# A decoder layer with 32 experts: the rings of raw expert weights hold two slots instead of three

## What is computed

```python
def _trunk_layer(x, mod, conv_buf, s0, lb, ...):
    u = x * (1.0 + scale1) + shift1
    p = u @ w_in                                   # short convolution | gated recurrence
    ...
    x = _layer_norm(DEEPNORM_ALPHA * x + gate1 * mix, ln_g[0], ln_b[0])
    u = x * (1.0 + scale2) + shift2
    y_moe = _hier_moe(u, w_rg, w_re, w_e_gate, w_e_up, w_e_down)
    x = _layer_norm(DEEPNORM_ALPHA * x + gate2 * y_moe, ln_g[1], ln_b[1])

def _grouped_experts(xt, eid, wts, w_gate, w_up, w_down):
    ...
    def expert_block(args):                        # a block is 128 rows of one expert
        xblk, ex = args
        h = jax.nn.silu(xblk @ w_gate[ex]) * (xblk @ w_up[ex])
        return h @ w_down[ex]
```

## Time and profile before

| | |
|---|---|
| median of 3 runs | 2151.04 us (2150.22 to 2154.14) |
| the profiled execution, its own time | 2152.77 us |
| its span (first to last instruction) | 2151.3 us |
| PE matmul | 1799.2 us, 84% |
| PE weight load | 1475.9 us, 69% |
| VectorE | 1194.1 us, 56% |
| ScalarE | 576.2 us, 27% |
| POOL (GpSimd) | 704.3 us, 33% |
| DMA | 342.19 MB, mean 159 GB/s |
| mean granted TensorE clock | 0.915 |

### The profile page before, as it was taken

How to read it: one execution, slowest core, us unless ns; L and a number is a source line. 1 busy time by engine, 2 the same in 40 slices (tenths; PEclk the granted TensorE clock), 3 DMA queues, 4 the chain that set the end, 5 groups by cost and what they waited for, 6 DMA issues and landing times. The chain is left out here.

```text
span 2151.3 us, 35708 instructions
## 1 busy us (share of the span) xinstructions
PE 1799.2 (84%) x11048; PEld 1475.9 (69%) x11049; DVE 1194.1 (56%) x1904; ACT 576.2 (27%) x795; POOL 704.3 (33%) x773
## 2 busy tenths in 40 slices
PE   6789998999989998999968999238999999999200
PEld 1179997999979997999957887106766667666000
DVE  2066665666666665566647765613455433354498
ACT  0032223222232223222221111103455434454000
POOL 1022221222222220222215444262344322344598
PEclk9989998999989998999989999568999999999555
DMA  6742223222222222222165443616899764895673
GB/s 214 244 123 73 80 70 115 62 83 83 81 87 69 78 83 72 70 83 74 54 217 189 150 150 111 241 30 217 294 344 359 287 218 168 272 327 207 273 272 138
DMA packets 274847, 342.19 MB, mean 159 GB/s; under 512 B 17975, under 2 KB 221752, under 8 KB 272364
## 3 DMA queue, kind: packets, MB, share of 16 engines
q1 hardware_dynamic: 242732, 256.43, 36.9%
q0 software_dynamic: 24592, 75.28, 9.6%
q10 hardware_dynamic: 7490, 10.08, 1.3%
HBM read 277.12 MB, written 64.62 MB: 159 GB/s over the span
## 5 line engine op out<-in xcount | busy, mean ns | idle before, releaser
L578 PE MATMUL pr<-u_hi,w_hi 128*128 128x264 f32 x1792 | 376.7, 292 | 17.4 <-DVE u_lo L732 13.1
L578 PE MATMUL pr<-u_lo,w_hi 128*128 128x264 f32 x1792 | 367.3, 287 | 0.0
L578 PE MATMUL pr<-u_hi,w_lo 128*128 128x264 f32 x1792 | 366.8, 286 | 0.0
L578 PEld LDWEIGHTS pr<-u_hi,w_hi 128*128 128x128 f32 x1792 | 281.0, 191 | 19.0 <-issue 13.5
L578 PEld LDWEIGHTS pr<-u_lo,w_hi 128*128 128x128 f32 x1792 | 281.0, 190 | 0.0
L578 PEld LDWEIGHTS pr<-u_hi,w_lo 128*128 128x128 f32 x1792 | 280.0, 190 | 0.0
L1220 DVE TENSOR_TENSOR w_gu_lo<-w_gu_raw,w_gu_hi (+1 forms) x64 | 146.3, 2290 | 145.2 <-ACT w_gu_hi L1213 139.1
L697 DVE TENSOR_TENSOR w_lo<-w_raw,w_hi 128x1024 fp32r<-128x1024 f32 x114 | 139.7, 1238 | 94.7 <-ACT w_hi L417 91.2
L1712 PE MATMUL ph<-w_gu_hi,x_hi 128*128 (+1 forms) x408 | 176.5, 433 | 11.4 <-DVE x_lo L1669 9.1
L1735 PE MATMUL py<-w_dn_w,hhT 128*128 x400 | 184.8, 605 | 0.5
L519 POOL TENSOR_TENSOR o_r<-o_ms,neg_half 128x5 f32<-128x5 f32 x16 | 19.1, 1196 | 476.7 <-DVE o_ms L846 476.7
(11 more groups left out here) (314 smaller groups left out, 3060.4 us busy)
## 6 DMA issues: line engine op xcount, KB each, us to landing
w_raw<-in_w_in SPq DMA_DIRECT2D x114, 512.0 KB, 4.0
w_gu_raw<-in_w_e_gate SPq DMA_DIRECT2D x32, 1024.0 KB
w_gu_raw<-in_w_e_up SPq DMA_DIRECT2D x32, 1024.0 KB
w_dn_w<-in_w_e_down SPq DMA_DIRECT2D x32, 1024.0 KB
w_ring<-in_w_mod SPq DMA_DIRECT2D x10, 2048.0 KB, 7.9
y_t<-y_scratch SPq DMA_DIRECT2D x16, 1024.0 KB, 5.1
x_rows<-in_x_prompt POOLq DMA_DIRECT2D x4, 2048.0 KB, 8.6
y_raw<-y_scratch SPq DMA_DIRECT2D x16, 512.0 KB, 4.9
```

The costliest lines, as they stand in the source:

```text
L578: last = pe.matmul(pr[j % 2][:, a * 512:a * 512 + HALF], w[:, s, k, :], x[:, k, a * HALF:(a + 1) * HALF], start=(k == 0 and n == 0), stop= ...
```

## The change

The constant RAW goes from 3 to 2, and the start of SyncE's loop in the expert phase is written with it (for RAW = 3 the new lines are the old ones).

```diff
@@ -47,7 +47,7 @@
-RAW = 3
+RAW = 2
@@ -1565,8 +1565,8 @@
                 sp.wait_ge(xg_in, 32)
-                gate_up(3, 0)
-                with sp.Fori(4, NE) as e:
+                gate_up(RAW, 0)
+                with sp.Fori(RAW + 1, NE) as e:
                     gate_up(e, sp.snap(e % RAW))
                     down(e - 1, sp.snap((e - 1) % RAW))
                 down(NE - 1, (NE - 1) % RAW)
```

## The result

The changed kernel takes 2163.03 us, the median of 12 runs (2157.07 to 2170.9), against 2151.26 us for 12 runs of the kernel before (2147.7 to 2155.74). The ratio is 1.0056, interval 1.0041 to 1.0070: slower by 11.8 us, where 8.0 was forecast. The profiled execution of the changed kernel took 2170.9 us, the slowest of its 12, over a span of 2169.4; that of before took 2152.77. So the two profiles differ by 18.1 us, more than the medians do. They show where the time goes, and exaggerate how much.

A forecast was written before the change was run, and what follows sets the result against it. TensorE bounds multi-block experts, weight loads at DMA pace the one-block streaks. Lateness of 4.7 + 4.2 = 8.9 us at most, 7.3 if shrunk, middle 8.0, on the 2151.04 us median gave 2159.0 us; range 2152.8 to 2165.5.

The forecast's parts named there:

- The shift by one expert: SyncE's queue: until a stall, each expert's load goes where before had the next expert's; same bytes and moments, one less ahead.
- The place: Only the two streaks of one-block experts grow, together 7 to 9 us; multi-block pieces keep 10.22 us a block.
- The terms of 4.7 and 4.2 us: ScalarE's split waits for late weights: 4.7 us at expert 13 in streak one, 4.2 us at expert 28 in streak two.
- After it the delay is carried along: Streak one: experts 14 to 17, 4.1 to 4.5 us late against before, are no longer late against the delayed order.
- Something comes back: In the streaks, delayed gathers and scatters leave DMA share to loads, shrinking 8.9 us to as little as 7.3; middle 8.0.
- The loads run at what the DMA gives: In streaks of one-block experts the weight loads set the pace, 10.87 us an expert at best.
- the cheaper slot index: Remainder by 2 drops one register instruction ahead of the first split on ScalarE and VectorE; taken as zero, bounded by 1.02 us.
- The slack of the down weights: Expert 10's down weights land by 1615.2, at least 4 us of cover, so PE does not wait at L1735.
- Routing: Routing stage: one expert's load fewer (3.15 MB), costed at nothing because POOL's list scatters set that stage.
- Absorbed: Rival: streak loads run at 10.87 us without slow pieces, costing 2 us, 2153.0, no change that can be told; chance 0.21.
- The closed cycle: Rival: in the streaks the two-slot load, split, free cycle binds, from a load of 13.3 us; 2171; chance 0.08.
- Faster through routing: Rival: the third load held POOL's routing scatters; dropping it returns 4.8 us, to 2146.2; chance 0.03.

The follow-up runs named there:

- first run: Kernel before with three slots kept, but SyncE's waits, routing loads and load order of the two-slot kernel: 2159.07 us, 1.0048 to the kernel before.
- ninth: The changed kernel unaltered, measured again on another chip: 2168.02 us, 1.0051 to the kernel before.
- tenth run: Changed kernel with gate and up loads issued apart, each behind its own landing, measured again beside the changed kernel: 2155.82 us, 1.0008 to the kernel before.
- sixth run: Kernel before, three slots, with gate and up loads issued apart, each behind its own landing: 2157.57 us, 1.0006 to the kernel before.
- twelfth run: Kernel before with two down slots, the down load one expert later, and each load behind its own landing: 2154.34 us, 0.9993 to the kernel before.
- fourth: Kernel before with three gate and up slots, two down slots, and the down load one expert later in SyncE's order: 2149.05 us, 0.9992.
- eighth run: Kernel before with three slots and all its waits, but only two experts loaded in routing: 2157.9 us, 1.0007 to the kernel before.
- eleventh run: Changed kernel, two slots, with gate and up loaded by halves, each behind its own landing and its own half slot: 2150.15 us, 0.9981 to the kernel before.
- second run: Changed kernel with two gate and up slots but three down slots: 2159.75 us, 1.0046 to the kernel before.

## Why the prediction was right, and where its sum fell short

**The shift by one expert** was right: the gate load of expert 11 is issued 0.13 us from where the one of 12 was before, the 3.57 us of the phases ahead taken off. The first run shows that it is the waits and not the memory.

**The place** was right: the multi-block pieces kept their pace (205.20 for 204.38 us; one step of 10.76 us makes most of the difference, in which ScalarE waited for POOL's row numbers). What grew are the two streaks, and in them ScalarE's idle time ahead of L1213, 5.54 and 3.08 us at experts 12 and 13 where 2 to 5 were expected. But it was expected for one or two experts, and came seven times in the first streak.

**The terms of 4.7 and 4.2 us** were near for the first lateness. The split of expert 13 comes at 1639.38, which is 4.3 us later than 1631.54 + 3.57. What failed is the step behind them, "After it the delay is carried along", and with it the step "Something comes back". The first took it that each further load keeps the pace that it had in before, the second even gave 0.9 us back because the loads would find less company. The runs showed the opposite sign: a load of the changed kernel took 11.85 us where one at the same place of before had taken 11.41. The issues, level at 1603.59, are 1698.40 - 1691.14 - 3.57 = 3.7 us behind at the end of the streak, and the blocks' delay grew from 4.3 us at expert 13 to 6.4. In streak two it is 7.8 for the 4.2. The mis-sized term is the sum of the two streaks, put at 8.0 us: it measured 11.8 in the medians, and 6.4 + 7.8 = 14.2 in the profiled execution, the longest of the twelve.

Its cause is shown by the pair of ninth and tenth run. Most landings leave a hole in the transfers, because the next load is issued only then. In before I had read the slow pieces of 12.1 to 12.6 us as something that comes with the order and that the change would inherit. With a wait of its own for each load they are gone: the sixth run, with three slots, has its gate loads 11.0 us apart throughout. The lead of three experts absorbs the hole; without the lead it is paid for. So the price of the missing slot is neither the lead alone (1 us is left in the tenth run, with an interval that takes in no change) nor the hole alone (nothing in the sixth and twelfth), but the two together.

**Two terms that the prediction had wrong, and that the total did not show.** The prediction let the loads set the pace of before ("The loads run at what the DMA gives"), and took the cheaper slot index as zero. The traces show another pace. With three gate slots the steady steps of a streak take 11.02 us, in before as in the fourth, sixth, eighth and twelfth run, however fast the loads come; with two they take 10.77 wherever no landing is waited for. A step of before, then one of the tenth run (whose lines are numbered two higher), in order of time:

```profile
1653.59 1.92 ACT L1213 ACTIVATE w_gu_hi<-w_gu_raw  x1 [1.02 <-DMA w_gu_raw<-in_w_e_gate]
1655.88 2.29 DVE L1220 TENSOR_TENSOR w_gu_lo<-w_gu_raw,w_gu_hi  x1 [4.56 <-ACT w_gu_hi L1213]
1660.06 2.28 DVE L1220 TENSOR_TENSOR w_gu_lo<-w_gu_raw,w_gu_hi  x1
1661.74 0.64 POOL L1611 COPY ids_cur<-ids_ring 128x4 int32 x1 [1.73 <-DMA y_scratch<-y_sb,ids_cur]
1662.48 1.12 ACT L1653 ACTIVATE y_sb<-py,ids_cur 128x1024 f32<-128x1024 f32 x1 [3.46 <-POOL ids_cur L1611]
1664.62 1.92 ACT L1213 ACTIVATE w_gu_hi<-w_gu_raw  x1 [1.03 <-DMA w_gu_raw<-in_w_e_gate]
```

```profile
1657.77 1.92 ACT L1215 ACTIVATE w_gu_hi<-w_gu_raw  x1 [0.91 <-issue]
1659.93 2.29 DVE L1222 TENSOR_TENSOR w_gu_lo<-w_gu_raw,w_gu_hi  x1 [4.32 <-ACT w_gu_hi L1215]
1664.10 2.28 DVE L1222 TENSOR_TENSOR w_gu_lo<-w_gu_raw,w_gu_hi  x1
1665.06 1.36 POOL L1613 COPY ids_cur<-ids_ring 128x4 int32 x1 [1.01 <-DMA y_scratch<-y_sb,ids_cur]
1666.52 1.12 ACT L1655 ACTIVATE y_sb<-py,ids_cur 128x1024 f32<-128x1024 f32 x1 [3.24 <-POOL ids_cur L1613]
1668.54 1.92 ACT L1215 ACTIVATE w_gu_hi<-w_gu_raw  x1 [0.90 <-issue]
```

The chain goes in a circle: ScalarE's split, VectorE's work from the first low split to the second, POOL's copy of the row numbers, `y_sb`, the next split. The copy ends 0.04 us after the second low split in both, whether it took 0.64 or 1.36 us; its row names the scatter's landing as what it waited for, but the low split is what it ends with. Two places differ: from the start of the split to that of the first low split it is 2.29 us and then 2.16, from the end of `y_sb` to the next split 1.02 and then 0.90. Together that is the 0.25 us of the step, and they are the two places at which a two-slot kernel has one register instruction less. The ring of down weights doesn't matter for it: with three gate slots and two down slots, in the twelfth run, the step is 11.02 us too. No run changes that instruction alone. The eleventh run, with two slots and no wait for a landing, has streaks of 106.99 and 74.69 us for 108.61 and 76.36: 3.3 us, most of what it gains on before. So the 1 us of the tenth run is a net figure: its price for the lead is larger, by what its shorter steps give back.

**The slack of the down weights** held: PE waited 3.2 us at L1735 in 3 waits, the longest 1.6. So the cover of 4 us did not hold everywhere. It mattered little: the second run, with three down slots, can't be told from the changed kernel (1.0046 beside 1.0056, each within the other's interval). **Routing** held: nothing gained, nothing lost that can be told.

**The rivals.** *Absorbed* was wrong, its condition did not come: the slow pieces were there again, more of them. The Trainium skill's rule behind it ("DMA: Bandwidth & Descriptors", section "Anatomy of one DMA") would move an expert's and a block's bytes in an estimated 9.6 us; that is the part by bytes alone, without the rule's 2 us for each transfer, and the section fits the rule to transfers issued by GpSimd, where the weights here are issued by SyncE. No run shows whether the 9.6 us can be had, since the best steps of 10.77 us are held by the chain above. At the 401 GB/s behind the tenth run's issues the 4.2 MB would take an estimated 10.5 us. *The closed cycle* came close without being the bound: loads of 13.0 to 13.4 us occur, at the 13.3 from which it decides, but three of the eight are 9.8 to 10.5, and SyncE's wait for a freed slot is 6.8 us in 9, the longest 1.0. *Faster through routing* was wrong in the changed kernel and in the eighth run, as it would be by the rule of "SBUF — State Buffer", section "Who interferes with whom", in the Trainium skill. The slow scatters stand again beside VectorE's four low splits, which the change left in place (8.90 us from 1400.38, the first slow scatter at 1400.59).

**What stays open.** Why two down slots in the old order cost more (1.0084) than two of everything (1.0056 and 1.0051); the intervals overlap, so the order of the two is not settled either. How the 11.8 us of the median divide over the streaks: the profile at hand is of the slowest execution, and before has a single profile too. How the 0.25 us of a step divide, and what the lead alone costs without them: no run has the waits of two slots, the hole closed and the slot index of three.

## What to carry to other kernels

A ring's lead is set by the queue that fills it, its order and what each issue waits for, and not by the number of slots alone; so look first at what stands behind a waiting issue. As long as a ring has lead to spare, a hole behind a landing costs nothing, and the day a slot is taken away it is paid for. Let each transfer wait for its own predecessor: here that bought back the slot within 1 us. Refilling the slot in the pieces in which it is freed and used took away the last waits. And close the circle of waits of one step and add it up, before you say that the loads set the pace: here two register instructions in it were worth 0.25 us a step.

## What the runs showed of the hardware

- In the 4 us behind a gate issue one core's DMA moved 401 GB/s on the mean of eight issues (374 to 421, tenth run) when the load was issued while the up load before it was still under way, and 300 (changed kernel beside it), 316 (changed kernel) or 355 (before) when it was issued only after that landing. Over a whole streak it moved 388 and 393 GB/s in the tenth and eleventh run, and 353 to 374 in the changed kernel and in before.
- TensorE's granted clock dipped where it had waited for weights: a mean of 0.80 from 1652.66 to 1656.66 us, so a part of it at the lower of its two levels (1.2 and 2.4 GHz), in a stretch in which it was busy 1.66 of 4 us. In the other windows of 4 us above it is 1.00. The matmuls of streak one kept it busy for 105.8 us in the changed kernel, 106.0 in its repeat, 104.7 in before and 104.1 in the tenth run: so with the waits the same matmuls count 1 to 2 us more of busy time. That the clock makes this difference is likely, and not shown apart.
- POOL's copy of the row numbers for `y_sb`, started beside VectorE's second low split, ended 0.04 to 0.06 us after that split: six of six between 1620 and 1690 us in before, though they took 0.42 to 1.15 us, and six of six in the eleventh run, at 0.43 to 1.98 us.
- POOL's copy of a block's row numbers (128 x 4) takes 0.19 us alone (at 1653.11 us in the changed kernel) and 1.41 us beside VectorE's low split (at 1642.46). Ten such copies make 14.9 us in before, and nine 7.2 in the changed kernel, where fewer of them stand beside a low split:

```profile
L1586 POOL COPY ids_now<-ids_ring 128x4 int32 x10 | 14.9, 1487 | 11.8 <-PE pxe L1700 6.7 <-DMA xg<-u_scratch,ids_now 5.1
...
L1586 POOL COPY ids_now<-ids_ring 128x4 int32 x9 | 7.2, 799 | 20.6 <-PE pxe L1700 20.6
```
